# Down product of a SwiGLU layer: the residual fetched in two groups, its first additions three tiles later, own banks for the seventh product

## The reference, cut to what matters

```
h = x
for layer in range(2):
    ...
    h = h + mix
    h = h + swiglu(rmsnorm(h, norm_ffn[layer]), w_gate, w_up, w_down)
return rmsnorm(h, norm_final)

def swiglu(u, w_gate, w_up, w_down):        # w_down: (2816, 1024)
    return (jax.nn.silu(u @ w_gate) * (u @ w_up)) @ w_down
```

## Time and profile before

| | |
|---|---|
| median of 3 runs | 2510.27 us (2509.97 to 2510.28) |
| the profiled execution | 2511.99 us |
| its span | 2510.0 us |
| TensorE busy | 2429.2 us, 97% of the span |
| VectorE busy | 1684.0 us, 67% |
| ScalarE busy | 1030.1 us, 41% |
| GpSimd busy | 523.2 us, 21% |
| mean granted TensorE clock | 0.981 |
| the chain that ended last | TensorE 88%, VectorE 6%, ScalarE 3%, DMA 2% |

### The profile page before, as it was taken

The page is one execution under the profiler, slowest core; times in us unless marked ns, Lnnn a source line. Parts: engine busy times, 40 slices in busy tenths (PEclk is TensorE's granted clock), DMA queues, the critical chain, the costliest instruction groups (busy, mean ns, idle before and its releaser), DMA issues.

```text
span 2510.0 us, 33612 instructions
## 1 busy us (share of the span) xinstructions
PE 2429.2 (97%) x12846; PEld 1912.4 (76%) x12846; DVE 1684.0 (67%) x2651; ACT 1030.1 (41%) x1810; POOL 523.2 (21%) x485
## 2 busy tenths in 40 slices
PE   9999999998999999999998999998999999999998
PEld 6587778875657788888886877776878888887886
DVE  5389966856644697777754478628578777765556
ACT  5423324545543343333333344438443333333334
POOL 5025533310000024343340000000004333332000
PEclk9999989998999999999999999998999999999999
DMA  6121100000004335555476651110335555557663
GB/s 193 44 68 43 42 26 10 2 35 1 1 25 126 134 127 167 168 168 168 168 260 226 197 158 44 51 35 25 93 118 176 168 168 168 168 183 291 196 197 113
DMA packets 236270, 298.25 MB, mean 119 GB/s; under 512 B 13424, under 2 KB 175232, under 8 KB 227024
## 3 DMA queue, kind: packets, MB, share of 16 engines
q1 hardware_dynamic: 220848, 207.66, 26.8%
q0 software_dynamic: 15264, 88.45, 9.3%
HBM read 206.95 MB, written 88.60 MB: 118 GB/s over the span
## 4 chain that ended last, share of the span: by engine, by line
PE 88%; DVE 6%; ACT 3%; DMA 2%; issue 2%; SPq 0%; POOL 0%; DVEq 0%; ACTq 0%; POOLq 0%
PE ps L371 24%; PE ps L372 23%; PE ps L373 23%; PE ps L3072 3%; PE ps L3049 2%; PE ps L3060 1%; DVE met L2197 1%; PE ps L2436 1%; ACT d_p L1707 1%; DMA hT<-park 1%; PE ps L2450 1%; PE ps L2445 1%; PE ps L1979 1%; PE ps L2489 1%; PE ps L2413 1%
## 5 line engine op out<-in xcount | busy, mean ns | idle before, releaser
L371 PE MATMUL ps<-ahi,whi 128*128 128x512 f32 x616 | 242.7, 394 | 18.1 <-DVE alo L1055 13.9
L371 PE MATMUL ps<-uhi,whi 128*128 128x512 f32 x608 | 244.8, 403 | 6.5 <-DVE ulo L530 3.4
L371 PE MATMUL ps<-q_T,whi 128*128 128x512 f32 x640 | 249.2, 389 | 1.6 <-ACT upr L852 1.6
L373 PE MATMUL ps<-q_T,wlo 128*128 128x512 f32 x640 | 249.0, 389 | 0.0
L372 PE MATMUL ps<-q_T,whi 128*128 128x512 f32 x640 | 249.0, 389 | 0.0
L371 PE MATMUL ps<-q_B,whi 128*128 128x512 f32 x608 | 238.9, 393 | 2.4 <-DVE q_B L530 2.4
L373 PE MATMUL ps<-ahi,wlo 128*128 128x512 f32 x616 | 241.0, 391 | 0.0
L372 PE MATMUL ps<-alo,whi 128*128 128x512 f32 x616 | 240.9, 391 | 0.0
L373 PE MATMUL ps<-uhi,wlo 128*128 128x512 f32 x608 | 237.0, 390 | 0.0
L372 PE MATMUL ps<-ulo,whi 128*128 128x512 f32 x608 | 237.0, 390 | 0.0
L373 PE MATMUL ps<-q_B,wlo 128*128 128x512 f32 x608 | 236.7, 389 | 0.0
(11 more groups left out here) (474 smaller groups left out, 5142.6 us busy)
## 6 DMA issues: line engine op xcount, KB each, us to landing
wraw<-in_ffn_w_gate_dram SPq DMA_DIRECT2D x44, 512.0 KB, 5.4
wd<-in_ffn_w_down_dram POOLq DMA_DIRECT2D x22, 1024.0 KB, 7.2
w_sums<-wd POOLq DMA_DIRECT2D x22, 1024.0 KB, 5.0
wraw<-w_sums SPq DMA_DIRECT2D x40, 512.0 KB, 3.8
araw<-act_sums SPq DMA_DIRECT2D x40, 512.0 KB, 4.6
wraw<-in_ffn_w_down_dram SPq DMA_DIRECT2D x30, 512.0 KB, 6.8
araw<-acts SPq DMA_DIRECT2D x30, 512.0 KB, 7.8
wraw<-in_ab_w_in_dram SPq DMA_DIRECT2D x24, 512.0 KB, 3.7
```

Of the source, the lines that this page charges most:

```text
L371: nc.tensor.matmul(dst, wh, xh, start=start, stop=False, **kw)
L373: return nc.tensor.matmul(dst, wl, xh, start=False, stop=stop, **kw)
```

## The change

The fetches of slices 0 to 3 stand behind the loads of tiles 5 to 8 and have one semaphore (`h_again`), those of slices 4 to 7 behind the loads of tiles 11 to 14 and have another (`h_rest`). The additions of product 0 stand behind the split of tile 10, those of product 2 begin with a wait for `h_rest`. The seventh product starts afresh in the other set of banks; what it used to find in its banks (the sum of products 1, 3 and 5) is added to its pieces by VectorE, four more additions in a layer (g = 6 of `ADDS`), and its own additions follow as g = 7. The sets of banks change places, so tile 0 takes its blocks in another order.

```diff
-    ((0, 1, 1), (1, 1, 1), 1, False, (1, 1)),
+    ((0, 1, 1), (1, 1, 1), 0, True, (1, 1)),
...
-DOWN_BANKS = ((6, 7, 0, 1), (2, 3, 4, 5))
-SAME_PIECE = {1: 0, 4: 3, 5: 2}
+DOWN_BANKS = ((6, 7, 4, 5), (0, 1, 2, 3))
+ADDS = [(i, d[4]) for i, d in enumerate(DOWN[:-1])] + [(5, (1, 1)), (6, (1, 1))]
+SAME_PIECE = {g: f for g in range(len(ADDS)) for f in range(g) if ADDS[f][1] == ADDS[g][1]}
+LAST_READ = {i: g for g, (i, _) in enumerate(ADDS)}
...
-                if 3 <= n < 3 + KT:
-                    if n == 3:
-                        sp_.wait_ge(*after("s_prod", NC * layer + AT[("S3", NJ - 1)] + 1))
-                    sp_.dma_start(hT[:, n - 3, :], park[:, n - 3, :]).then_inc(S("h_again"), 16)
+                if n == 5:
+                    sp_.wait_ge(*after("s_prod", NC * layer + AT[("S3", NJ - 1)] + 1))
+                if 5 <= n < 9:
+                    sp_.dma_start(hT[:, n - 5, :], park[:, n - 5, :]).then_inc(S("h_again"), 16)
+                if 11 <= n < 15:
+                    sp_.dma_start(hT[:, n - 7, :], park[:, n - 7, :]).then_inc(S("h_rest"), 16)
...
-                for q in range(len(pairs)):
-                    if i == len(DOWN) - 1 and c == 1 and q == 1:
-                        norm_whole(pe, 2 * norm + 2, DOWN_BANKS[0][0])
+                blocks = [(q, m) for q in range(len(pairs)) for m in range(4)]
+                if n == 0:
+                    blocks.sort(key=lambda b: b[1] // 2)
+                for q, m in blocks:
+                    if i == len(DOWN) - 1 and c == 1 and (q, m) == (1, 0):
+                        pe.wait_ge(*after("d_added", 4 * len(ADDS) * layer + 4 * 6 + 1))
+                        norm_whole(pe, 2 * norm + 2, DOWN_BANKS[1][0])
...
+                    if c == 0 and q == 0 and earlier:
+                        pe.wait_ge(*after("d_added", 4 * len(ADDS) * layer + 4 * LAST_READ[earlier[-1]] + m + 1))
+                    elif c == 0 and q == 0 and (i, m) == (0, 2):
+                        pe.wait_ge(*out_count(layer, "C12", NJ - 1))
...
-                if n % DC == 1:
-                    i = n // DC - 1
-                    if i == 0:
-                        dve.wait_ge(*after("h_again", 16 * KT * (layer + 1)))
-                    if i < 5:
-                        for m in range(4):
-                            h_add(i, m)
+                if n == DC + 4:
+                    dve.wait_ge(*after("h_again", 64 * (layer + 1)))
+                    for m in range(4):
+                        h_add(0, m)
+                if n == 3 * DC + 1:
+                    dve.wait_ge(*after("h_rest", 64 * (layer + 1)))
+                if n % DC == 1 and 2 <= n // DC <= 5:
+                    for m in range(4):
+                        h_add(n // DC - 1, m)
...
+            h_add(6, 0)
             norm_add(dve, 2 * norm, KT - 1)
             down_low(last + 2)
+            for m in range(1, 4):
+                h_add(6, m)
             down_low(last + 3)
             norm_invert(dve, 2 * norm)
...
-                h_add(6, m)
+                h_add(7, m)
...
-                     {(0, 0): after("d_added", 20), (1, 0): after("d_added", 26)})
+                     {(0, 0): after("d_added", 28)})
```

More of the change, by code:

```diff
@@ L783, in down @@
                 pe.wait_ge(*after("a_lo", DT * layer + n + 1))
-                for q in range(len(pairs)):
-                    if i == len(DOWN) - 1 and c == 1 and q == 1:
-                        norm_whole(pe, 2 * norm + 2, DOWN_BANKS[0][0])
-                    cols = slice(q * HALF, (q + 1) * HALF)
-                    for m in range(4):
[L789 to L801, removed]
@@ new lines, in down @@
+                blocks = [(q, m) for q in range(len(pairs)) for m in range(4)]
[5 more added lines that the diff above has]
+                        norm_whole(pe, 2 * norm + 2, DOWN_BANKS[1][0])
+                    cols = slice(q * HALF, (q + 1) * HALF)
+                    if c == 0 and q == 0 and earlier:
+                        pe.wait_ge(*after("d_added", 4 * len(ADDS) * layer + 4 * LAST_READ[earlier[-1]] + m + 1))
+                    elif c == 0 and q == 0 and (i, m) == (0, 2):
+                        pe.wait_ge(*out_count(layer, "C12", NJ - 1))
+                    w = slice(q * HALF + m * P, q * HALF + (m + 1) * P)
+                    last = three_pass(bank(banks[m]), whi[:, tile.slot, w], wlo[:, tile.slot, w],
+                                      ahi[:, n % RING, cols], alo[:, n % RING, cols],
+                                      start and c == 0 and q == 0, c == DC - 1 and q == len(pairs) - 1,
+                                      skip_group_check=True)
+                    if c == DC - 1 and m < 3:
+                        last.then_inc(S("d_part"), 1)
@@ L880, in square @@
             def square(v, k):
-                act.wait_ge(*after("d_added", 4 * len(DOWN) * layer + added_at(k, v % 2)))
+                act.wait_ge(*after("d_added", 4 * len(ADDS) * layer + added_at(k, v % 2)))
                 norm_square(act, v, k)
@@ L921, in ffn_act @@
             down_high(last + 3)
-            norm_root(act, 2 * norm, DOWN_BANKS[0][0], True)
+            norm_root(act, 2 * norm, DOWN_BANKS[1][0], True)
             down_high(last + 4)
@@ L1062, in h_add @@
                     tile_done(dve, down_tile(layer, DC * (i + 1) - 1))
-                if i in SAME_PIECE:
-                    dve.wait_ge(*after("d_added", 4 * len(DOWN) * layer + 4 * SAME_PIECE[i] + m + 1))
-                half, h = DOWN[i][4]
+                if g in SAME_PIECE:
+                    dve.wait_ge(*after("d_added", 4 * len(ADDS) * layer + 4 * SAME_PIECE[g] + m + 1))
+                half, h = ADDS[g][1]
                 dst = hT[:, 4 * half + m, rows_of(h)]
@@ L1349, in turn @@
                 if j < 6:
-                    pe.wait_ge(*after("d_added", 4 * len(DOWN) + (20 if j < 2 else 23 + j)))
+                    pe.wait_ge(*after("d_added", 4 * len(ADDS) + (28 if j < 4 else 27 + j)))
                 else:
```

8 lines of the change are left out of this document (4 added, 4 removed).

## The result

The changed kernel takes 2485.81 us (median of 4 runs, 2485.4 to 2489.31), the kernel before 2510.12 us beside it (4 runs): ratio 0.9903, 95% interval 0.9891 to 0.9916, so 24.3 us less. The forecast was 2489.5 us with a range of 2486.5 to 2493.5. The same kernel run again later (e3) gave 2488.15 us beside 2512.3 us for the kernel before, 24.15 us less: the time moved by 2.3 us and the saving hardly at all. Executions of the kernel before differ by more than the 0.31 us of its first three: fifteen beside e1 lie between 2508.46 and 2514.49 us. One execution of e7 took 9113.74 us, for no reason that the record shows, and counts nowhere here.

A forecast was written before the change was run, and what follows sets the result against it. TensorE, busy 97% of the span, was taken as the bound, so only its pauses and slow stretches could be saved: 17.6 + 2.9 + 0.3 = 20.8 us, giving 2489.5 us, range 2486.5 to 2493.5.

The forecast's parts named there:

- The pauses at tile 8: Down products: TensorE's pause and the slow matmuls behind it go, 11.05 us in layer 0 and 6.57 in layer 1.
- No new wait behind tile 10, at the narrow tile 11 or at the banks of tile 12: Down products: the moved fetches and additions finish before TensorE needs their results, over 3.4 us of cover; cost zero.
- B: Rival: DMA limits, so a pause remains at tiles 6 to 10; 2494.0 or 2490.5 us, chance 0.12.
- D: Rival: the wait moves with the additions behind tile 10, making tile 11 late; 2507 us, chance 0.02.
- The start: Down product's first tile: bank 4 is free 1.8 us early, cost zero; without the reordering about a microsecond.
- The seventh product: End of the down product: bank waits of 2.93 us a layer go, gaining 2.9 us in layer 1, 0.3 in layer 0.
- rival A: All of the seventh product's pause is won in both layers; 2486.9 us, chance 0.10.
- The clock at the transition: Layer 0 to layer 1: TensorE's expected pauses of 1.6 and 0.9 us bring no lower clock; cost nothing.
- Rival C: The lower clock (1.2 GHz) comes in at layer 0's transition, costing 1.9 us; 2491.4 us, chance 0.07.
- The sum: Whole kernel: 17.6 + 2.9 + 0.3 = 20.8 us off the span, 2510.0 to 2489.2, the rest unchanged.

The follow-up runs named there:

- e3: The changed kernel run again, nothing altered: 2488.15 us, ratio 0.9908.
- e1: The kernel before with only the two groups of fetches and the first additions behind tile 10, seventh product's banks as before: 2494.5 us, ratio 0.9933.
- e7: The changed kernel with eight extra matmuls (1.81 us) ahead of product 2 in layer 0: 2488.16 us, ratio 0.9907.
- e4: The changed kernel with all eight fetches behind tiles 3 to 10 in one group, as before; first additions still behind tile 10: 2486.76 us, ratio 0.9902.
- e9: The changed kernel with the first additions back behind the split of tile 7, the two groups of fetches kept: 2489.38 us, ratio 0.9914.
- e10: The changed kernel with the blocks of tile 0 in their plain order: 2489.7 us, ratio 0.9912.
- e5: The kernel before with eight extra matmuls (1.81 us) ahead of product 2 in layer 0: 2510.72 us, ratio 0.9997.
- e6: The changed kernel with four extra matmuls (0.91 us) ahead of product 2 in layer 0: 2489.73 us, ratio 0.9913.
- e2: The kernel before with only the seventh product's banks changed, its four additions and tile 0's new order; fetches and first additions as before: 2506.6 us, ratio 0.9981.
- e8: The changed kernel with some sums of squares and the low split of layer 1's first weights made earlier, for a shorter transition: 2487.86 us, ratio 0.9904.

## Why the prediction was off, point by point

- **The pauses at tile 8** (17.6 us): right. 11.1 and 6.6 us in e1. That the slow matmuls behind the pauses go with them was right too.
- **No new wait behind tile 10, at the narrow tile 11 or at the banks of tile 12**: right; rivals B and D did not happen. The cover was larger than I counted on, as e4 and e9 show.
- **The start**: zero with the new order, right. "Without the reordering it would be about a microsecond" was wrong: 0 and 0.4 us (e10). The prediction's own rows said so for layer 0: six matmuls behind 1289.24 is 1290.60, and the sum ended at 1290.13.
- **The seventh product** (2.9 us in layer 1, 0.3 in layer 0): right, 2.95 and 0.23. VectorE's chain in layer 0 took the four additions into its own pauses and stayed as long as it was, so TensorE gave back at the transition what it won at the banks, and rival A did not happen there.
- **The clock at the transition**: 1.00. Rival C did not happen. The Trainium skill, "TensorE: Matmul & The Clock Gate", Part 1, ties the clock to recent activity; here two pauses of 1.4 and 0.75 us, 8 us apart, did not bring the lower level in.
- **The sum: the step that failed.** It set "span 2510.0 - 20.8" and "the tail behind it ... moves along unchanged". The stages touched gave 20.9 us. The rest of the program did not keep its time, and the prediction had put that at nothing without a reason: 1.6 us in layer 1's output product and 0.8 in its attention products, in all five profiles with the change's down products and nothing added, and in neither of the kernel before. In the output product they are about eight matmuls at the lower level. e5 and e6 show that a shift is enough: work added some 400 us ahead took the slow matmuls out of the product in one kernel and brought them into it in the other, while the product and the wait of 2.03 us ahead of it stayed the same. Each of the two is one profile.
- **What about the shift decides it stays open.** The output product took 90.5 to 90.6 us when it began at 1737.2, 1740.7, 1744.7, 1746.7 or 1748.9, and 89.0 when it began at 1734.4, 1735.6, 1736.1, 1736.2, 1736.6, 1738.2, 1739.0, 1739.1 or 1750.0; nothing between. So its time in the span does not sort the cases: 1737.2 is slow between 1736.6 and 1738.2, and two executions of the kernel before are both slow 2.2 us apart. The same page of the Trainium skill says in Part 1 that the activity check runs freely and does not start anew with a kernel. These profiles neither show nor refute that; they show slow stretches that lie at no fixed time in the span and, by e2, not always at the start of the stage.
- **What else stays open.** By the medians 20.9 + 2.4 = 23.3 of the 24.3 us are accounted for, and 1.0 is not. By the two profiles 2.4 of the 25.7 us are left, and they lie in the tail (1.3), layer 0's output product (0.6) and the time ahead of the delta stage (0.5). No run tells a scatter between executions from an effect of the change there. Why the delta stage has more or fewer slow matmuls from one execution to the next (420.2 to 421.7 us, or 424.6) was not tried.
- **The range** left 3 us below the forecast, all given to rival A. It had no term for the clock of untouched stages. With 2 to 3 us for that it would have begun near 2484. The time is a borderline miss (2485.81 in one set of runs, 2488.15 in the other, both sets together 2486.7 against a bound of 2486.5); the saving is not, 24.3 and 24.15 us where 20.8 were summed.

## What to carry to other kernels

A wait for a transfer in the middle of an engine's queue holds up all that is queued behind it, and costs something when part of that is due before the transfer lands: 11.52 us of waiting cost 9.2 us of TensorE's time, 4.29 us cost nothing (e9). Issue the transfer in the groups in which it is used, or put its first user behind work that is due sooner; here either alone took all of the pause. When matmul stages sit behind short waits, an edit elsewhere can add or remove slow matmuls in them; here shifts of 0.9 and 1.8 us did, and up to 2.4 us hung on it. So compare kernels stage by stage between fixed instructions, and give the sum an allowance for that. A gain of 2.6 us like that of e8 can only be seen in its own stage.

## What the runs showed that I had not expected

- 1.81 us more TensorE work made the kernel before no slower: 2510.72 against 2511.35 us.
- VectorE waited 4.29 us for a transfer without any cost, and four more additions left its chain in layer 0 as long as it was (11.93 against 11.97 us).
- One and the same kernel has a delta stage of 421.6 or 424.6 us from one execution to the next, at a granted clock of 0.83 or 0.77 in 60 us of it. That is more than half of the 4.5 us that its runs scatter.
